# Attention in a two-block transformer kernel: value products with the values as weights, and the division by the sum moved to the probabilities

## What is computed

```python
def first_block(x, ...):                       # 2 layers
    h = rms_norm(x, norm_pre_mix[l])
    mix = hybrid_mixer(h, ...)                 # 8 heads of dilated attention (64 wide) + 4 gated-delta heads
    x = x + rms_norm(mix, norm_post_mix[l])
    x = x + rms_norm(conv_glu_ffn(rms_norm(x, ...)), ...)

def second_block(x, positions, ...):           # 2 layers
    q, k, v, iq, ik, iw = ...                  # 8 heads of 64
    score = sum_h iw[h] * relu(iq[h] @ ik.T)   # an index score per query and key, causal by chunks of 64
    top_idx = top_k(score, 128)                # each query attends to its 128 best keys
    p = softmax(q @ k[top_idx].T * 64 ** -0.5);  o = p @ v[top_idx]
    ...
```

## Time and profile before

| | |
|---|---|
| time, median of 3 runs | 2942.12 us (2939.2 to 2942.17) |
| the profiled execution | 2941.83 us, span 2940.0 us |
| mean granted TensorE clock | 0.972 of full |
| TensorE matmul / VectorE / ScalarE / GpSimd busy | 95% / 41% / 38% / 42% of the span |
| attention stages | 108 to 221.5 us, 887.5 to 1001, 1760 to 1836, 2437 to 2512 |

### The profile page before, as it was taken

The page is one execution under the profiler, slowest core; times in us unless marked ns, Lnnn a source line. Parts: engine busy times, 40 slices in busy tenths (PEclk is TensorE's granted clock), DMA queues, the critical chain, the costliest instruction groups (busy, mean ns, idle before and its releaser), DMA issues.

```text
span 2940.0 us, 44118 instructions
## 1 busy us (share of the span) xinstructions
PE 2802.6 (95%) x15368; PEld 2235.2 (76%) x15368; DVE 1202.5 (41%) x2246; ACT 1129.4 (38%) x1950; POOL 1223.6 (42%) x630
## 2 busy tenths in 40 slices
PE   9998999999999989999999889999999998999997
PEld 7777777888877777888888567778788666778776
DVE  4555455551256553655403774410113685410012
ACT  4454244443335533444423326432323325432331
POOL 3313135554432222355544451364553451264553
PEclk9999999999999989999999999999999999899998
DMA  3211012223221101222232120122222120122222
GB/s 128 73 50 37 9 65 92 93 93 101 92 82 58 58 9 37 72 93 94 99 105 76 58 72 30 55 94 95 93 93 74 58 79 30 43 92 95 93 93 93
DMA packets 62874, 217.25 MB, mean 74 GB/s; under 512 B 6576, under 2 KB 6704, under 8 KB 62480
## 3 DMA queue, kind: packets, MB, share of 16 engines
q1 hardware_dynamic: 62416, 214.28, 22.3%
q0 software_dynamic: 320, 1.12, 0.2%
HBM read 213.28 MB, written 2.10 MB: 73 GB/s over the span
## 4 chain that ended last, share of the span: by engine, by line
PE 79%; DVE 8%; ACT 4%; POOL 4%; issue 3%; DVEq 1%; ACTq 0%; POOLq 0%
PE bank L1819 51%; POOL wL L742 4%; PE bank L2139 3%; PE bank L1868 2%; PE bank L1846 2%; PE bank L2048 2%; PE bank L1996 2%; PE bank L1997 2%; PE bank L1998 2%; ACT wH L912 2%; PE bank L2037 1%; PE bank L2025 1%; PE bank L1876 1%; DVE bias L1696 1%; PE bank L1935 1%
## 5 line engine op out<-in xcount | busy, mean ns | idle before, releaser
L742 POOL TENSOR_TENSOR wL<-raw,wH 128x1024 fp32r<-128x1024 f32 x380 | 920.8, 2423 | 1255.2 <-ACT wH L912 1254.9
L1819 PE MATMUL bank<-hH,wH 128*128 128x512 f32 x1744 | 722.4, 414 | 30.4 <-POOL wL L742 17.1
L1819 PE MATMUL bank<-hL,wH 128*128 128x512 f32 x1744 | 686.0, 393 | 0.0
L1819 PE MATMUL bank<-hH,wL 128*128 128x512 f32 x1744 | 684.8, 393 | 0.0
L912 ACT ACTIVATE wH<-raw 128x1024 fp32r<-128x1024 f32 x380 | 399.5, 1051 | 264.0 <-PE bank L1819 236.1
L1819 PEld LDWEIGHTS bank<-hH,wH 128*128 128x128 f32 x1744 | 330.7, 190 | 151.8 <-issue 57.9
L1819 PEld LDWEIGHTS bank<-hH,wL 128*128 128x128 f32 x1744 | 331.3, 190 | 71.3 <-issue 10.3
L1819 PEld LDWEIGHTS bank<-hL,wH 128*128 128x128 f32 x1744 | 330.3, 189 | 71.9
L1819 PE MATMUL bank<-hidH,wH 128*128 128x512 f32 x864 | 337.6, 391 | 2.4 <-POOL wL L742 2.4
L1819 PE MATMUL bank<-hidH,wL 128*128 128x512 f32 x864 | 336.2, 389 | 0.0
L1819 PE MATMUL bank<-hidL,wH 128*128 128x512 f32 x864 | 336.2, 389 | 0.0
(11 more groups left out here) (328 smaller groups left out, 3871.0 us busy)
## 6 DMA issues: line engine op xcount, KB each, us to landing
raw<-w_dram SPq DMA_DIRECT2D x398, 512.0 KB, 3.3
x<-x_dram SPq DMA_DIRECT2D x4, 512.0 KB, 9.4
out_dram<-x SPq DMA_DIRECT2D x1, 2048.0 KB, 6.2
const<-const_dram SPq DMA_DIRECT2D x1, 1229.0 KB, 14.1
par_next<-par_dram POOLq DMA_DIRECT2D x5, 168.0 KB, 2.6
qkT<-pos_dram POOLq DMA_DIRECT2D x1, 256.0 KB, 7.1
const<-const_dram SPq DMA_DIRECT2D x1, 131.0 KB, 2.2
```

The source lines that it names most:

```text
L742: pool.tensor_tensor(wL[:, s, :], raw[:, s, :], wH[:, s, :].bitcast(F32), ALU.subtract).then_inc(w_lo.sem, 1)
L1819: mm = pe.matmul((out or ACC[bk])[:, :], wt[:, s, c:c + P], rhs, start=first and k == 0 and j == 0, stop=last and k == tiles - 1 and j == 2)
```

## The change

The values become the weights, and the turned probabilities stream. The output of a head then comes out already transposed, 64 rows high, and the two heads of a pair write the lower and the upper 64 partitions of `TRO` directly. So `OA`, `ao`, ScalarE's scaled copy and the transpose of outputs are no longer used here. Columns of the result are now queries, so a per-query factor can't be applied on the way out. VectorE therefore multiplies the probabilities by the reciprocal of their sum, in place, before they are transposed. TensorE's transposes wait for that (`rsum`) and no longer for exp alone (`prob`). The value products of a pair are made together, in every odd slot from 3 on, ahead of the transposes of that slot.

```diff
 # ScalarE, attention(w, n)
                     if m >= 2:
-                        act.wait_ge(pv_done.sem, pv_done.at(w, m - 1))
+                        act.wait_ge(pv_done.sem, pv_done.at(w, m - m % 2))
                     wd = P * (att_step(m)[1] + 1)
                     act.activation(pt[:, m % 2, 0:wd], PT[:, 0:wd], ACT.Copy).then_inc(pt_copied.sem, 1)
-                m = n - 2
-                if 0 <= m < 32:
-                    c, p = m % 4, m // 2
-                    act.wait_ge(pv_done.sem, pv_done.at(w, m + 1))
-                    act.wait_ge(rsum.sem, rsum.at(w, m + 1))
-                    if p >= 2:
-                        act.wait_ge(tro_done.sem, tro_done.at(w, p - 1))
-                    act.activation(ao[:, p % 2, m % 2 * HD:m % 2 * HD + HD], OA[:, 0:HD], ACT.Copy,
-                                   scale=st[:, RS + c:RS + c + 1]).then_inc(oa_read.sem, 1)
 # VectorE, attention(w, n), behind the minimum of step n
                     dve.wait_ge(prob.sem, prob.at(w, m + 1))
-                    dve.reciprocal(st[:, RS + c:RS + c + 1], st[:, SUM + c:SUM + c + 1]).then_inc(rsum.sem, 1)
+                    wd = P * (att_step(m)[1] + 1)
+                    dve.reciprocal(st[:, RS + c:RS + c + 1], st[:, SUM + c:SUM + c + 1])
+                    dve.drain()
+                    dve.tensor_scalar(sc[:, m % 2, 0:wd], sc[:, m % 2, 0:wd], st[:, RS + c:RS + c + 1], None,
+                                      ALU.mult).then_inc(rsum.sem, 1)
                 if n % 8 == 2 and n >= 10:
                     f = (n - 10) // 8
-                    dve.wait_ge(tro_done.sem, tro_done.at(w, 4 * f + 4))
+                    dve.wait_ge(pv_done.sem, pv_done.at(w, 8 * f + 8))
 # TensorE, attention(w, n, fill)
                 for i in fill[0:1]:
                     half_step(w, i // 4, i % 4, 0)
+                if n >= 3 and n % 2:
+                    p = (n - 3) // 2
+                    f, i, _ = att_step(2 * p)
+                    pe.wait_ge(pt_copied.sem, pt_copied.at(w, 2 * p + 2))
+                    if p % 4 == 0 and p >= 4:
+                        pe.wait_ge(piece_ready.sem, piece_ready.at(w, n0 + p // 4))
+                    for j in range(i + 1):
+                        for h in range(2):
+                            mm = pe.matmul(TRO[h * HD:h * HD + HD, f * P:f * P + P],
+                                           v[:, j, (2 * f + h) * HD:(2 * f + h) * HD + HD],
+                                           pt[:, h, j * P:j * P + P], start=j == 0, stop=j == i)
+                    mm.then_inc(pv_done.sem, 2)
                 m = n - 1
                 if 0 <= m < 32:
                     f, i, h = att_step(m)
-                    pe.wait_ge(prob.sem, prob.at(w, m + 1))
+                    pe.wait_ge(rsum.sem, rsum.at(w, m + 1))
                     if m:
                         pe.wait_ge(pt_copied.sem, pt_copied.at(w, m))
...
-                m = n - 2
-                if 0 <= m < 32:
-                    f, i, h = att_step(m)
-                    pe.wait_ge(pt_copied.sem, pt_copied.at(w, m + 1))
-                    if m:
-                        pe.wait_ge(oa_read.sem, oa_read.at(w, m))
-                    for j in range(i + 1):
-                        mm = pe.matmul(OA[:, 0:HD], pt[:, m % 2, j * P:j * P + P],
-                                       v[:, j, (2 * f + h) * HD:(2 * f + h) * HD + HD], start=j == 0, stop=j == i)
-                    mm.then_inc(pv_done.sem, 1)
-                if n >= 4 and n % 2 == 0:
-                    p = (n - 4) // 2
-                    pe.wait_ge(oa_read.sem, oa_read.at(w, 2 * p + 2))
-                    if p % 4 == 0 and p >= 4:
-                        pe.wait_ge(piece_ready.sem, piece_ready.at(w, n0 + p // 4))
-                    pe.transpose(TRO[:, p % 4 * P:p % 4 * P + P], ao[:, p % 2, :], ident).then_inc(tro_done.sem, 1)
```

More of the change, by code:

```diff
@@ L469, in build @@
         pv_done = signal("pv_done", 32, 32)
-        oa_read = signal("oa_read", 32, 32)
-        tro_done = signal("tro_done", 16, 16)
         conv_in = signal("conv_in", 12, 0)
```

## The result

The changed kernel takes 3052.8 us (median of 4 runs, 3048.2 to 3054.5), the kernel before on the same chip 2942.1: a ratio of 1.0365, with an interval from 1.0333 to 1.0397. The forecast was 3042, the range 2990 to 3085, slower with a chance of 0.95. The profiled execution took 3051.4 us, 109.6 more than that of before; its span is 3049.6.

A forecast was written before the change was run, and what follows sets the result against it. TensorE was taken as the bound in all four attention stages. Terms -24 + 44 + 12 + 16 + 20 + 8 + 10 - 1 = +85, plus 15 for the clock, +100 on 2941.8 us: 3042 us, range 2990 to 3085.

The forecast's parts named there:

- Even slots of block 1: Block 1 attention: transposes wait 1.12 to 1.72 us for VectorE's division behind the new minimum; 22 us a layer, 44 us.
- GpSimd in the way: Block 1: five multiplications a layer wait for GpSimd's 2.4 us subtractions on a shared port; 8 us a layer, 16 us.
- Odd slots: Block 1: division mostly covered by the joint value step; 0.3 us a slot, 1.7 in slot 1; 12 us.
- TensorE's own work: Value products and output transposes removed, joint steps added: 5.8 us less a layer, 24 us less over four.
- Clock: Block 1 attention: nine falls to 0.50 of the granted clock after long TensorE idles, about 1.7 us each; 15 us.
- Block 2: Block 2 attention: waits before transposes 20 us, GpSimd blocks 8 us, joint step waiting for ScalarE's copy from slot 17 10 us.
- no port, no clock: Rival: the waits before transposes are there, but neither GpSimd nor the clock adds; 3003 us, chance 0.15.
- the clock falls after nearly every wide wait: Rival: 1.68 us idle suffices, so twenty more falls of 1.7 us; 3076 us, chance 0.15.
- halves in series: Rival: column halves of joint value steps do not overlap in long runs, 8.8 us a layer more; 3077 us, chance 0.05.
- waits are partly taken up: Rival: VectorE and ScalarE run ahead while TensorE stands; a third of waits gone, no clock loss; 2990 us, chance 0.13.

The follow-up runs named there:

- Experiment 6: Changed kernel with the exponential written to the freed PSUM bank and VectorE's multiplication reading it there instead of in SBUF; 3034.8 us, 1.0333.
- experiment 5: Changed kernel with small constant products on TensorE between scores and transposes of block 1's even slots, to fill idle time; 3042.4 us, 1.0336.
- experiment 1: Changed kernel without the multiplication, so probabilities are not divided by their sum and transposes wait for exp; 2929.3 us, 0.9950.
- experiment 4: Changed kernel with GpSimd's subtraction in five units of block 1 made to wait for the multiplication it held; 3028.2 us, 1.0284.
- Experiments 3: Changed kernel with VectorE's reciprocal and multiplication of step n-1 put ahead of the minimum of step n; 2970.6 us, 1.0092.
- experiment 9: Kernel of Experiments 3 with two more block 1 divisions moved, between the convolution's second and third parts and ahead of the silu; 2964.7 us, 1.0083.
- kernel of 11: Kernel of experiment 9 with each block 2 GpSimd subtraction of half weights held until the multiplication it would block is done; 2943.0 us, 1.0008.

## Why the prediction was right, point by point

Signs and mechanism were right, and so were the places of the waits; the clock also fell where the sum has nothing for it. The total came 10 us too low, and that it came so near is in part luck, since block 1 was taken too high and block 2 too low. By the terms of the sum:

- **Even slots of block 1** (44 us): right. From scores to transposes at 128 keys 1.32 us, without the division 0.20, so 1.12; at 512 keys 2.24 against 0.52, 1.72. These are the two ends that the earlier trace rows gave. The eleven even slots without a block stand idle for 14.6 and 14.2 us in the two layers, for which the interpolation gave 14.8.
- **GpSimd in the way** (16 us): right in number, steps and price. The five waits are 14.7 us a layer against 15.4 from 7.4 of even slots and 8 of blocks. By the Trainium skill, "SBUF — State Buffer", section "Who interferes with whom", a tensor_scalar in a 2-port mode waits for the whole of a GpSimd instruction that came first. The trace agrees but for 0.2 us: the 2.28 us multiplication, 0.29 us alone, ends 0.08 us behind the subtraction. Experiment 6 agrees too, where with a PSUM source it runs inside.
- **Odd slots** (12 us): 7, since the waits were 3.5 and 3.8 us a layer and not 6. It was the roughest value, between 0 and 0.65 a slot. More than half of what is missing was there and went into the falls: in experiment 5, with no fall, the odd slots wait 5.1 and 5.0 us.
- **TensorE's own work** (-24 us): too large. A block 1 layer without the division is 3.4 us shorter, not 5.8. The joint steps have the lengths that I gave them, at all four widths. Of the missing 2.4 us, 1.4 are no work but a wait: the kernel of experiment 1 stands 2.3 us a layer before the sums of the norm, the kernel before 0.9, the changed one not at all. The work itself is 4.8 less; the last 1.0 was not traced.
- **Clock** (15 us, nine falls in block 1): eight falls there, worth 9 us by experiment 5. The 1.7 each is the work that a fall takes; the sum had not seen that a wait behind it gives some back. They are also why TensorE's busy time in block 1 rose, where I had said it would be shorter.
- **Block 2** (25 us by the terms, with TensorE's share): 40.8, the part that was undersized. The waits were right: before transposes they rose by 14.2 and 14.5 us a layer (14 taken), before the joint step by 5.3 (5 taken, from slot 17 on, as said). What failed is the clock term, which I had placed in block 1 alone. Block 2 begins with falls already, and its stages were at the low level for 16.7 and 12.5 us before, 22.3 and 23.8 after: half of the difference is 8.5 us. With the waits, 39.3, that makes 47.8, so 7.0 of the 12 us of TensorE's saving are left. By the same account the kernel of experiment 1 saves 5.3 and 6.8 us a layer in block 2, so the saving itself was not too large there; what took the other 5 us in the changed kernel is open.

So block 1 came to 67.4 where the terms say 75, block 2 to 40.8 where they say 25: two errors of opposite sign. Checked against the runs, block 1 closes: 65.6 of waits before the transposes, 9.7 less of work (4.8 to 4.9 a layer, experiment 1), 1.9 less of waits before the norm's sums, and eight times 1.7 for the falls, 13.6, are 67.6. The 9.0 of experiment 5 must not be added to these waits, since what the falls took from them is already gone from the 65.6.

Of the rivals, "no port, no clock" fell with experiment 4, "the clock falls after nearly every wide wait" with the counts (unblocked waits of 1.45 to 1.81 us, as they stand alone in experiment 4, left it up; in the changed kernel one of 1.81 had a fall behind it), "halves in series" with the row of 0.80 us, and "waits are partly taken up" holds only in small: a third of what the falls in block 1 cost.

What I had not seen is that the loss is no property of the change. Experiments 3, 9 and 11 do the same work in another order, step by step down to 2943. The minimum, the convolution and the silu ahead of the division on VectorE, and subtractions released without regard to it, make up the 110 us between that kernel and the changed one.

## What to carry to other kernels

When an operation is moved onto the path of the bounding engine, its own 0.3 to 0.5 us are the small part. Read what stands ahead of it in the queue of its engine in the slot where it is now needed, and put it there as soon as its operand is ready, neither before (the engine then stands, and others wait for it) nor behind work that can wait. A VectorE multiplication out of and into SBUF that another engine waits for should not meet a long GpSimd instruction (where none waits, as for four of the five in block 1 of experiment 9, it costs nothing). If it is on the path, hold GpSimd behind it, count the step that the hold waits for against the trace, and look at old multiplications too, which a shift can push into the same place.

## What the hardware showed that was not expected

- A multiplication with a PSUM source is not held by GpSimd: 0.35 us inside a subtraction of 2.39, against 2.28 with an SBUF source at the same step. The convolution's parts, one operand in SBUF and one in PSUM, are not held either. In the kernel of 11:

```profile
210.03 2.39 POOL L740 TENSOR_TENSOR wL<-raw,wH 128x1024 fp32r<-128x1024 f32 x1 [9.30 <-ACT wH L911]
...
210.12 1.57 DVE L1425 SCALAR_TENSOR_TENSOR xb<-bank,par,xb 128x511 f32<-128x511 f32 x2
```

- Where falls of the clock come: in block 1 of experiment 4, whose longest waits are 1.5 to 1.8 us every few slots, there are none; in experiment 6, with waits up to 2.0 us, two a layer; in the changed kernel, with 2.5 to 3.5, three to five. One of its falls (193.1) came behind a wait of 1.81 us, while the 2.90 us before step 11's transposes brought none in either layer. The same stage in two layers of the changed kernel, with waits equal to 0.2 us in sum, had five falls and three.
- A fall of 3.41 us at 0.50 costs 1.6 us where TensorE would not have waited soon after, and 0.7 to 1.2 where it would (1.1 in the mean of eight), as the engine that TensorE waits for keeps its pace.
